# HGRN heads: VectorE's reciprocals placed elsewhere, and both parts of the joined pairs of levels 2 and 4 next to each other on TensorE

## What is computed

```
proj = h @ w_in                  # q, fl, iv, g
f = lb + (1 - lb) * sigmoid(fl);  k = 1 - f
per block:  bcum = cumsum(log f)
  scores[t,s] = sum_k q[t,k] k[s,k] exp(bcum[t,k] - bcum[s,k])      (s <= t)
  o = scores @ i + (q * exp(bcum)) @ s
  s = exp(b_last) * s + (k * exp(b_last - bcum))^T @ i
o = o * rsqrt(mean(o*o) + eps) * norm_w * silu(g);   out = o @ w_o
```

## Time and profile before

| | us |
|---|---|
| median of 3 runs | 2634.57 (2631.55 to 2636.13) |
| profiled execution, its own time | 2633.32 |
| its span, first to last instruction | 2631.5 |
| TensorE matmuls busy in it | 2566.3 |
| VectorE busy | 2189.0 |
| GpSimd busy | 1495.6 |
| ScalarE busy | 963.3 |
| mean granted TensorE clock | 0.995 of full |

### The profile page before, as it was taken

One profiled execution on the slowest core, in us unless ns is written; L12 is line 12 of the kernel. 1 busy time (PEld: TensorE's weight loads), 2 busy tenths in 40 slices (PEclk: granted clock), 3 DMA queues, 4 the chain that ended last, 5 costly groups with the idle time before them and its releaser, 6 DMA issues. The chain is left out here.

```text
span 2631.5 us, 50936 instructions
## 1 busy us (share of the span) xinstructions
PE 2566.3 (98%) x21184; PEld 2496.5 (95%) x21184; DVE 2189.0 (83%) x2653; ACT 963.3 (37%) x1593; POOL 1495.6 (57%) x1184
## 2 busy tenths in 40 slices
PE   8999999999999999999999999989999999999998
PEld 8999899999999999999888889879999999999998
DVE  8887768999999898766877777897899999989875
ACT  4012635444444433331222122233544444442433
POOL 5223586777777569862121212128577777756995
PEclk9999999999999999999999999999999999999999
DMA  5333253122222523221111111125322222243221
GB/s 158 69 67 65 86 200 107 69 75 76 76 76 76 206 89 121 67 112 49 50 42 50 50 42 50 43 74 200 121 76 76 76 76 76 76 183 112 90 98 73
DMA packets 162421, 235.40 MB, mean 89 GB/s; under 512 B 77584, under 2 KB 112400, under 8 KB 162192
## 3 DMA queue, kind: packets, MB, share of 16 engines
q1 hardware_dynamic: 81680, 158.36, 18.1%
q10 hardware_dynamic: 80512, 73.78, 8.4%
HBM read 172.91 MB, written 59.20 MB: 88 GB/s over the span
## 5 line engine op out<-in xcount | busy, mean ns | idle before, releaser
L1283 PE MATMUL BANKS<-XB_A,OPS 128*128 128x288 f32 x3432 | 510.3, 297 | 0.3 <-ACT U L2285 0.3
L1283 PEld LDWEIGHTS BANKS<-XB_A,OPS 128*128 128x128 f32 x3432 | 473.0, 189 | 4.1 <-issue 1.7
L1283 PE MATMUL BANKS<-XB_B,OPS 128*128 128x288 f32 x2904 | 437.1, 296 | 0.0
L1283 PEld LDWEIGHTS BANKS<-XB_B,OPS 128*128 128x128 f32 x2904 | 403.3, 189 | 0.0
L998 POOL TENSOR_TENSOR SMALL<-WRAW 128x1 f32<-128x1 f32 x76 | 21.5, 283 | 667.4 <-PE BANKS L1605 426.8
L3053 DVE SCALAR_TENSOR_TENSOR C<-U,HGA,C 128x1168 f32<-128x1168 f32 x176 | 273.7, 1575 | 35.8 <-ACT C L2304 34.3
L1028 POOL TENSOR_TENSOR OPS<-RAW,OPS 128x512 fp32r<-128x512 f32 x126 | 164.3, 1316 | 200.3 <-ACT OPS L2211 200.3
L1028 POOL TENSOR_TENSOR OPS<-TMP,OPS 128x512 fp32r<-128x512 f32 x168 | 223.3, 1338 | 50.2 <-ACT OPS L2211 50.2
L3125 DVE TENSOR_TENSOR X<-BANKS,X 128x576 f32<-128x576 f32 x224 | 167.8, 750 | 68.2 <-PE BANKS L1377 67.8
L2211 ACT ACTIVATE OPS<-TMP 128x512 fp32r<-128x512 f32 x168 | 106.2, 633 | 283.5 <-POOL TMP L1022 180.2
L1605 PE MATMUL BANKS<-XH,WH 128*128 128x384 f32 x744 | 190.5, 357 | 3.9 <-DVE HGA L3212 2.5
(11 more groups left out here) (372 smaller groups left out, 5853.4 us busy)
## 6 DMA issues: line engine op xcount, KB each, us to landing
RAW<-in_w SPq DMA_DIRECT2D x84, 512.0 KB, 4.4
WRAW<-in_w SPq DMA_DIRECT2D x68, 512.0 KB, 3.6
g_kept<-C ACTq DMA_DIRECT2D x44, 512.0 KB, 2.6
x_kept<-X ACTq DMA_DIRECT2D x24, 576.0 KB, 3.0
XB_BF<-x_kept SPq DMA_DIRECT2D x16, 576.0 KB, 8.6
XB_BF<-g_kept SPq DMA_DIRECT2D x32, 288.0 KB, 4.6
WAY_BF<-g_kept SPq DMA_DIRECT2D x32, 288.0 KB, 4.8
WRAW<-in_w SPq DMA_DIRECT2D x32, 256.0 KB, 3.4
```

Source lines behind the costliest of these rows:

```text
L1283: ins = nc.tensor.matmul(out[:, cols], w[:, a, p, :], x[:, b, cols], start=s in OPENS and p == 0 and q == 0, stop=p == PAIRS - 1 and q == ...
```

## The change

The reciprocals of the norm of head h - 1 go to other places in VectorE's order. In heads 1 to 7 `own` stands ahead of the first of them, not behind it. In heads 1 to 5 the second goes from behind `own` to ahead of `stream_values`, and the third stays behind `stream_values`. In head 6 the second takes the place of the third, and the third and `normed` go behind `key(7)`. In head 7 `gated(6)` and the second go behind `picks(4, "B")`, and the third behind `states`.

On TensorE one piece of a large product, which stood between the parts A and B of the pairs of levels 2 and 4, now stands ahead of part A. For level 2 that piece is row 0 of the next unit; for level 4 it is the last rows of the unit (rows 6 and 7 in heads 0 to 5, row 4 in heads 6 and 7). No instruction is added, removed or altered.

```diff
 (TensorE, heads 0 to 5)
+                part("V", h + 1, 0, 1)
                 joined(2, "A", h)
-                part("V", h + 1, 0, 1)
                 joined(2, "B", h)
                 part("V", h + 1, 1, 3)
                 values(h)
                 part("V", h + 1, 3, 6)
+                part("V", h + 1, 6, KD)
                 joined(4, "A", h)
-                part("V", h + 1, 6, KD)
                 joined(4, "B", h)
 (head 6)
+            part("F", h + 1, 0, 1)
             joined(2, "A", h)
-            part("F", h + 1, 0, 1)
             joined(2, "B", h)
             part("F", h + 1, 1, 4)
+            part("F", h + 1, 4, 5)
             joined(4, "A", h)
-            part("F", h + 1, 4, 5)
             joined(4, "B", h)
 (head 7)
+            part("G", h, 0, 1)
             joined(2, "A", h)
-            part("G", h, 0, 1)
             joined(2, "B", h)
             part("G", h, 1, 2)
             values(h)
             part("G", h, 2, 4)
+            part("G", h, 4, 5)
             joined(4, "A", h)
-            part("G", h, 4, 5)
             joined(4, "B", h)
 (VectorE, the loop over heads)
+                own(h)
                 if h:
                     inverse(h - 1, 0)
-                own(h)
-                if h:
-                    inverse(h - 1, 1)
                 first_level(h)
...
+                if 0 < h < HEADS - 2:
+                    inverse(h - 1, 1)
                 stream_values(h)
                 if 0 < h < HEADS - 2:
                     inverse(h - 1, 2)
...
                 projected("F", h + 1, FG)
                 if h == HEADS - 2:
-                    inverse(h - 1, 2)
+                    inverse(h - 1, 1)
                 picks(6, "A", h)
                 joined_raised(6, h)
                 picks(6, "B", h)
-                if h == HEADS - 2:
-                    normed(h - 1)
                 forget(h + 1)
                 key(h + 1)
+                if h == HEADS - 2:
+                    inverse(h - 1, 2)
+                    normed(h - 1)
                 states(h)
...
             h = HEADS - 1
-            dc.inc(gated(h - 1))
             picks(4, "A", h)
-            inverse(h - 1, 2)
             joined_raised(4, h)
             picks(4, "B", h)
+            dc.inc(gated(h - 1))
+            inverse(h - 1, 1)
             projected("G", h, GATE)
...
             states(h)
+            inverse(h - 1, 2)
             normed(h - 1)
```

## The result

The changed kernel takes 2645.47 us in the median of five runs (2642.92 to 2649.69), against 2634.57 before (five runs, 2631.55 to 2639.38). The ratio is 1.0044, with a 95% interval of 1.0033 to 1.0055: 10.9 us slower. The profiled execution's span is 2643.0 us, 11.5 more than before, so the trace can be used for the whole difference.

The account below looks back on a forecast made before the run. TensorE, busy 98% of the span, was taken as the bound. Terms: -0.65 + 0.65 + 2.24 - 1.05 + 1.3 + 2.6 + 0.5 + 1.1 = +6.7 us, giving 2641.3 us on the median; range 2633.5 to 2644.5.

Parts of the forecast that it names:

- Parts 1 and 2: Heads 1 to 5: own's earlier start is eaten by the late J2A and moved reciprocal; gain 0.13 us a head, about 0.65.
- rival (c): Heads 1 to 5: VectorE reads V out by 1449.2, saving 1.5 us a head; 2634.4 us in all, chance 0.12.
- Part 3: Head 0: V's row 0 held 1.5 us, J4A leaving V gives 0.8 back; +0.65 us.
- Part 4: Head 6: J2A waits behind F's row 0, so picks(2,A) and TensorE's Q row come late; +2.24 us, bounds 0 and 2.6.
- Part 5, head 7: Head 7: 1.05 us of the lateness won back, then 1.3 lost to the clock; +0.25 us.
- The stall of J6A: Head 7: J6A's wait of 4.33 us goes, as GpSimd's subtraction comes later, at 1731.5.
- the sum takes gated first: Head 7: gated starts at 1731.40, ahead of GpSimd's subtraction at 1731.5; the other order would add 2.4 us.
- rival (b): Head 7: GpSimd's subtraction gets ahead of gated(6); +2.4 us on top, 2643.7 us, chance 0.12.
- The clock term behind it: Head 7: half clock around and after TensorE's wait ahead of the output product; +1.3 us.
- rival (a): Last head and tail: TensorE's clock stays up in the moved waits; +4.3 us, 2638.9 us in all, chance 0.2.
- Part 5, the tail: After keys(7): reciprocal ahead of normed 2.6 us, longer low parts 0.5, half clock at the sums 1.1.

Follow-up runs that it names:

- e4: Changed kernel with row 0 of V, F or G put back between J2A and J2B in all heads; 2631.39 us.
- e3: Kernel before with VectorE's new order in heads 1 to 5 alone; 2627.4 us.
- e7: Kernel before with VectorE's new order in heads 1 to 5 and J4A directly ahead of J4B in heads 0 to 5; 2623.55 us.
- e5: Changed kernel with F's row 0 put back between J2A and J2B in head 6 alone; 2641.24 us.
- e1: Kernel before with TensorE's half of the change alone; 2640.74 us.
- e6: Changed kernel with gated(6) moved behind the reciprocal that followed it; 2644.77 us.
- e8: Changed kernel with five spare products in TensorE's wait ahead of F's row 0 in head 6; 2647.8 us.
- e10: Changed kernel with reciprocal 2 of head 7 ahead of states; 2640.68 us.
- e9: e7 with VectorE's new order in head 7 too, but the last reciprocal ahead of states; 2621.4 us.
- e2: Kernel before with VectorE's half of the change alone; 2630.64 us.

## Why the prediction was right or wrong, part by part

**Parts 1 and 2, heads 1 to 5: right, in size and in mechanism.** No wait ahead of scores(1) or J2A, V's row 0 held (0.96 us of wait, then 1.28 us for its first three products, where the prediction had 1.4 or more), 2.23 us of idle VectorE ahead of picks(2,A) (forecast 2.2), no gap ahead of the V projection, -0.2 us a head against -0.13. The prediction's account that the reciprocals' gain is eaten by the late J2A is shown by e4: without it the head is 70.42. The moved reciprocal, which it named beside it, eats next to nothing by itself (e3: 1.2 of 1.29 us arrive). Both gains named there, VectorE's and the 0.8 of J4A, exist with the sizes of e3 and e7, 1.2 and 0.77, and row 0 takes 1.76 back. This is also why rival (c) failed: VectorE reads V out from 1451.93, which is 1450.5 in the times of the trace before (1.4 less), as forecast (1450.55), not by 1449.2. Its price was 1.5 us a head; with row 0 left behind J2A the gain is 1.96.

**Part 3, head 0: right,** +0.8 for +0.65. With J4A's gain alone it is 0.79 shorter (e7), so row 0 ahead of J2A costs 1.6 there, forecast 1.5.

**Part 4, head 6: the mechanism right, the term mis-sized,** +4.3 for +2.24, with bounds of 0 and 2.6 that did not hold it. e5 gives the whole to row 0 ahead of J2A, as forecast. The step that failed is to have priced the new wait by its end alone. TensorE stands still for 2.55 us there, where it is 0.96 in heads 1 to 5, since behind scores(1) only two rows of V stand ahead of it and not three of G (1.57 us a row), and the clock fell behind it: 1.1 us. The prediction spoke of the clock in head 7 only. The other 0.8 is a VectorE product that now meets GpSimd's cast (1672.53 against 1672.61); that part is in all five traces of this order in head 6 (after, e1, e6, e8, e10), the clock's part is not: without it the term would have been 3.1.

**Part 5, head 7: wrong in one step,** +2.2 for +0.25. The stall of J6A went as forecast: it waits 0.23 us in place of 4.33. What failed is "the sum takes gated first". Gated and GpSimd's subtraction began within 0.01 us of each other, and VectorE was held: rival (b). Its price, +2.4, was right (3.58 - 1.41 = 2.2 in the row, 2.1 for head 7 in e6); its chance of 0.12, with a margin of 0.1 us between two starts summed over ten slots, was too low. The sum could not tell the order, and it took the two starts for independent, while the traces have them in step, with VectorE held in five of five. The clock term behind it held: the half level from 1740 to 1746, in two rows of TensorE by stretch,

```profile
1740.00:1742.00 2.00, 0.00 (x0) 0.00 (x0) 1.90 (x5) 0.00 (x0) 0.00 (x0) 0.50 0.00 0
...
1744.00:1746.00 2.00, 2.00 (x8) 2.00 (x7) 1.97 (x7) 0.00 (x0) 0.00 (x0) 0.50 0.00 0
```

and rival (a), that the clock stays up, did not occur there.

**Part 5, the tail: right in sum,** +4.1 for +4.2, less so in its terms. VectorE, then TensorE:

```profile
1757.16 1.36 DVE L3370 TENSOR_TENSOR X<-HGA,X 128x1152 f32<-128x1152 f32 x1
...
1764.63 8.01 DVE L3411 TENSOR_TENSOR XL<-X,XH 128x1152 fp32r<-128x1152 f32 x4
...
1764.82 0.77 PE L1701 MATMUL BANKS<-HGA,CONST 128*128 128x128 f32 x2 [4.19 <-DVE HGA L3406]
1765.38 3.62 PE L1756 MATMUL BANKS<-HGA,CONST 128*128 128x512 f32 x4
```

From keys(7) to the low parts it is 17.40 us (1747.23 to 1764.63) against 14.84 (1740.01 to 1754.85): +2.6, the reciprocal, exactly the term. The four low parts take 8.01 in place of 6.66, +1.35 for the 0.5 taken, inside its bounds. Of the 1.1 for the clock only 0.2 is left to add behind VectorE (4.1 - 2.6 - 1.35), although the sums do take 3.62 us at the half level. Two misses of about 0.9 cancel, by luck.

**The sum.** Forecast +6.7, in the trace +10.4 for HGRN: 2.0 more in head 6, 1.9 more in head 7, the rest within 0.3. No forecast case held rival (b) and a clock stretch in head 6 together.

## What to carry to other kernels

A product that is put ahead of another one must not be waiting for a slower thing than the other one is: row 0 waited for a read-out, J2A for a pick that came first, and TensorE's fixed order handed the read-out's delay on to the pick's whole chain (1.76 us a head, enough to hide the 1.96 that the other two moves brought). Try the parts of a change alone before giving it up; here the other moves of heads 0 to 5, with the last head's reciprocals placed once more, make the kernel 0.5% faster (e9). And where two engines hold each other up, look at the start times of the pair: a plan with a margin of a tenth of a microsecond doesn't give the order, the first trace does, and moving one instruction by one place changes it (2.1 us in e6).

## What the runs showed of the hardware

**A TensorE wait of 1.7 to 2.6 us may or may not cost the clock.** The first wait of head 6 is 2.11 us in e3 and 2.10 in e7, in the same code of that head. In e3:

```profile
1647.39 0.63 PE L1684 MATMUL BANKS<-X,HGA 128*32 128x48 f32 x40 [2.11 <-DVE HGA L3242]
...
1650.00:1652.00 2.00, 2.00 (x37) 1.45 (x36) 0.94 (x3) 0.00 (x0) 0.00 (x0) 0.50 0.75 252
```

and in e7:

```profile
1643.09 0.63 PE L1684 MATMUL BANKS<-X,HGA 128*32 128x48 f32 x40 [2.10 <-DVE HGA L3242]
...
1644.00:1646.00 2.00, 1.98 (x29) 1.47 (x32) 2.00 (x6) 0.00 (x0) 0.94 (x1) 1.00 0.09 18
```

In e3 the half level follows the wait and head 6 is 1.4 us longer; in e7 nothing follows, nor in the other five traces with this wait (before, e2, e4, e5, e9). The same holds at the end: the wait of 2.2 us ahead of sums(7) left the clock up before, in e1 and in e9 (sums in 1.88 us) and brought it down in e3, e7 and e10 (3.43, 3.29 and 2.71), in the first two for 0.7 us of tail. In head 6 of the changed order the 2.56 us ahead of F's row 0 cost nothing in e10 and 1.1 us in the changed kernel, and the fall came at the following wait, of 1.69 us, in e6 and e8. So a wait's length did not decide it here. What does is not settled: each of these kernels has one trace, and no run repeated one of them to see whether it falls at the same place twice. But the executions of one kernel differ too: the ten of e3 run from 2624.72 us to 2633.94, at mean granted clocks of 0.996 and 0.994, with 0.998 the highest and 0.993 the lowest between them. A forecast can take such a wait only as a cost between 0 and about 2.3 us (66.89 against 64.58 in head 6). The half level came with each of the 18 waits of 4.17 us and more in this stage of the twelve traces.

**One VectorE instruction, two prices.** The same gated(6) takes 1.32 us when it comes behind GpSimd's subtraction (e6), 1.41 when it starts 0.03 us ahead of its cast (e2, e9; then the cast takes 2.27 for 1.03), and 3.58 when it and the subtraction start at once (after, e4, e5, e8, e10). The profile's start times don't say which of the two was held, since VectorE's row begins at the tie and contains its wait; the lengths do.
